# The program's beginning of a two-layer decoder: c spread into PSUM, six modulation rows on TensorE

## The chip, the cores and the metric

One core of one Trainium2 chip runs the whole program, as one launch. The time is device microseconds (us), the median of several executions.

## The reference, cut to what matters

Two layers (HGRN2, then forgetting attention), each followed by a squared-ReLU MLP, over 512 tokens of width 1024 in float32. Every sub-layer begins with an RMSNorm whose result is scaled and shifted by values that come from one conditioning vector c:

```python
c_act = jax.nn.silu(c)
for i in range(DEPTH):
    mod = c_act @ w_mod[i] + b_mod[i]          # (1, 6 * 1024)
    sh1, sc1, g1, sh2, sc2, g2 = jnp.split(mod, N_MOD, axis=-1)
    h = rmsnorm(x, norm1_w[i]) * (1 + sc1[:, None, :]) + sh1[:, None, :]
    ...
    proj = h @ w_in                            # hgrn2: q, fz, i, g
```

For the first projection the program thus needs the norm of x, and of `mod` the 1024 shifts sh1 and the 1024 scales sc1.

## The kernel before, in words

Activations lie transposed: tile `x` has 128 partitions by 8 feature blocks (k = 0 to 7) by 512 tokens. A weight comes as blocks of 128x1024 (512 KB). Products are made to near float32 accuracy out of a high and a low part: a matmul of `whi` with `h0hi`, of `whi` with `h0lo` and of `wlo` with `h0hi` (lines 704 to 706, 128x512 each), so that every block and every k costs three matmuls. ScalarE makes the high part of a weight block (`whi`), VectorE or GpSimd the low part (`wlo`).

Each engine has its order written out by hand, and semaphores join them. The DMA queue of SyncE loads in program order: c spread over all partitions (`cb`), the parameters (`par`), x, then the rows of w_mod in `modf` (first_rows(k) loads rows k and 8 + k), among them the first four weight blocks.

The beginning, up to the first projection's four blocks (`together`), works in these steps:

- The norm. ScalarE squares the eight blocks of x (L377), VectorE adds seven of them into `acc` (L1278), TensorE sums over partitions with matmuls of one column (`norm_0`, L732 and L736), VectorE adds epsilon (L1171), GpSimd takes the root (`root`, L648), TensorE spreads it over the partitions into a PSUM bank (L741).
- The modulation. Row m of `modf` holds, in partition p, the 1024 weights of output 128 m + p, so an output is a dot product along the free dimension with the silu of c in `cb`. VectorE takes the 8 shifts and the first 3 scales (L1262, `first_dots`), the other 5 scales are a product on GpSimd (L656) and a sum on ScalarE (L388). VectorE then adds the bias (L1268) and makes the gain (L1270).
- h0 itself, block by block of k: `t_of_0` (L1176, x times gain times root, the root read from PSUM) into one of two `scr` buffers; ScalarE adds the shift and rounds (L383, `h0hi`); `lower_0` (L1181) is the low part.
- TensorE waits for `h_lo` of k and runs 12 matmuls (four blocks by three).

GpSimd has in its queue, in this order: eight constants, seven masks (built in `scr[1]`, L626 to L636), the root, the low parts of the first four weight blocks (`lo`, L644), the five products of scales. VectorE waits for `masked` before `t_of_0(0)`.

After the four blocks come the value blocks of the next quad (L795 to L797), then the HGRN2 levels (`hg_core`), which other code orders. SyncE's queue goes on with a wait on `w_lo` before each reload of a weight buffer.

Of the kernel before, what the change touches and what calls it, by code (L numbers as in the profile page):

```python
# [13 lines left out]
P = 128  # L14
T = 512
# [23 lines left out]
C_ALL = C_BMOD + 96  # L39
# [3 lines left out]
SPLITS = 10  # L43


def build(nc, x_t, c_row, stream, mod_rows, w_forget, params, out_t):
    keep = ExitStack()
    with keep:
# [15 lines left out]
        dots = sb("dots", [P, 4], F32)  # L64
        qkw = sb("qkw", [P, 1], F32)
# [16 lines left out]
        lbc = sb("lbc", [P, 6 * KT], F32, layer0)  # L82

# [3 lines left out]
        modf = sb("modf", [P, 2 * KT, D], F32, head0)  # L87
        head0.close()
# [39 lines left out]
        x_in = [sem(f"x_in{i}") for i in range(2)]  # L128
        par_in, wf_in, c_in = (sem(n) for n in ("par_in", "wf_in", "c_in"))
        modf_in = [sem(f"modf_in{i}") for i in range(KT)]  # L130
# [5 lines left out]
        cact = sem("cact")  # L136
# [8 lines left out]
        n_sum, n_var, n_rst, n_bc = (sem(n) for n in ("n_sum", "n_var", "n_rst", "n_bc"))  # L145
        h_t, h_hi, h_lo = (sem(n) for n in ("h_t", "h_hi", "h_lo"))
# [21 lines left out]
        SHARED = 3  # L168

# [6 lines left out]
        SQ_AT = {1: 8, 2: 20, 3: 30, 4: 42}  # L176
        ADD_AT = {1: 7, 2: 16, 3: 23, 4: 32}
# [101 lines left out]
        def _(sp):  # L279
            sp.dma_start(cb[:, :], c_row.partition_broadcast(P)).then_inc(c_in, 16)  # L280
            sp.dma_start(par[:, :], params).then_inc(par_in, 16)
            for i in range(2):
                sp.dma_start(x[:, 4 * i:4 * i + 4, :], x_t[:, 4 * i:4 * i + 4, :]).then_inc(x_in[i], 16)
            def first_rows(k):

                rows = mod_rows[0:2 * KT].rearrange("(h m) p k -> p h m k", h=2)
                sp.dma_start(modf[:, :, :].rearrange("p (h m) k -> p h m k", h=2)[:, :, k, :],
                             rows[:, :, k, :]).then_inc(modf_in[k], 16)
# [52 lines left out]
        def _(act):  # L341
# [259 lines left out]
        def _(pool):  # L601
# [17 lines left out]
            n = 6  # L619
            for lv in range(MASKED):  # L620
                pool.wait_ge(gp, n)
                if lv:
                    m = 1 << (lv - 1)
                    nb = P // (2 * m)
                    v = scr[1][:, 0:P].rearrange("p (b h m) -> p b h m", h=2, m=m)
                    G.memset(v[:, :, 0, :], 0.0)  # L626
                    G.memset(v[:, :, 1, :], 1.0).then_inc(gp, 1)

                    pool.wait_ge(gp, n + 1)
                    G.affine_select(out=v[:, :, 1, :], in_=v[:, :, 1, :], compare_op=ALU.is_ge, fill=0.0,  # L630
                                    base=0, pattern=[[-2 * m, nb], [0, m]], channel_multiplier=1).then_inc(gp, 1)
                    pool.wait_ge(gp, n + 2)
                    G.affine_select(out=v[:, :, 1, :], in_=v[:, :, 1, :], compare_op=ALU.is_gt, fill=0.0,
                                    base=m, pattern=[[2 * m, nb], [0, m]], channel_multiplier=-1).then_inc(gp, 1)
                    pool.wait_ge(gp, n + 3)
                    G.tensor_copy(masks[:, lv, :], scr[1][:, 0:P]).then_inc(gp, 1)  # L636
                    n += 4
            pool.wait_ge(gp, n)
            G.memset(scr[1][:, 0:1], 0.0).then_inc(masked, 1)
# [11 lines left out]
            for j in range(4):  # L651
                lo(0, j)
            pool.wait_ge(cact, 1)
            for k in range(SHARED, KT):
                pool.wait_ge(modf_in[k], 16)
# [40 lines left out]
        def _(pe):  # L696
# [29 lines left out]

            def norm_0():
# [94 lines left out]
            def together(jobs, h, ready):  # L822

                for k in range(KT):
                    pe.wait_ge(h_lo, ready + k + 1)
                    for quad, j, bank in jobs:
                        if k == 0:
                            split(quad, j)
# [877 lines left out]
```

## Time and profile before

| | us |
|---|---|
| median of 3 runs (lowest 1471.47, highest 1475.01) | 1474.58 |
| the profiled execution | 1476.3 |
| its span, first to last instruction | 1474.5 |
| TensorE matmul busy in the span | 1399.3 (95%) |
| VectorE busy | 774.9 (53%) |
| ScalarE busy | 501.6 (34%) |
| GpSimd busy | 162.5 (11%) |
| mean granted TensorE clock | 0.979 |

The page of the profile gives the busy time of each engine over the whole span and then in 40 slices of 37 us. Of the first slice PE is busy two tenths, VectorE seven, GpSimd eight, and the DMA engines nine; of every later slice PE is busy eight tenths or more, and the last has seven. Times of the trace run from the span's start. The page calls TensorE PE, VectorE DVE, ScalarE ACT, GpSimd POOL and SyncE SP. A matmul of 4-byte operands that are not fp32r (the sums, the spreads, the dots) is listed as two instructions, each with its own load of the stationary operand, so that x8 stands for four of them in the code.

### The profile page before, as it was taken

How to read it: one execution, taken by the hardware profiler on the slowest of the kernel's cores; microseconds unless marked ns; L12 is line 12 of the kernel's file. 1: busy time of each engine (PE TensorE's matmuls, PEld its weight loads, DVE VectorE, ACT ScalarE, POOL GpSimd, SP SyncE). 2: the span in 40 equal slices, each digit the busy share in tenths (PEclk: the TensorE clock that was granted, in tenths of full speed). 3: DMA queues.
4: the chain of work that ended last, by engine and by line, in shares of the span. 5: the costliest groups of instructions: out<-in, count | busy, mean ns of one | idle time of the engine just before them, and what ended most of it. 6: DMA issues, size and time to landing. Idle time of an engine off the chain costs nothing.

```text
span 1474.5 us, 21837 instructions
## 1 busy us (share of the span) xinstructions
PE 1399.3 (95%) x8152; PEld 1217.8 (83%) x8152; DVE 774.9 (53%) x1348; ACT 501.6 (34%) x771; POOL 162.5 (11%) x199
## 2 busy tenths in 40 slices
PE   2899999999999999999998898998999999999997
PEld 2688988989988888888997797987899888888887
DVE  7865757565775556653464454454466433244323
ACT  3423232413443223332253444444344322133220
POOL 8242415050000000000020101010000000000000
PEclk9899999999999999999999999999999999999999
DMA  9243334322365446542232121211023322323221
GB/s 374 100 167 130 116 115 140 119 72 58 106 243 179 171 180 230 189 170 85 73 105 97 57 87 58 86 51 51 29 86 101 100 86 85 108 92 99 88 69 58
DMA packets 47224, 169.95 MB, mean 115 GB/s; under 512 B 5025, under 2 KB 7201, under 8 KB 46385
## 3 DMA queue, kind: packets, MB, share of 16 engines
q1 hardware_dynamic: 46544, 164.73, 32.7%
q10 hardware_dynamic: 608, 4.23, 0.7%
q8 instruction: 50, 0.82, 0.2%
q14 instruction: 22, 0.17, 0.0%
HBM read 166.81 MB, written 2.13 MB: 115 GB/s over the span
## 4 chain that ended last, share of the span: by engine, by line
PE 87%; DVE 6%; ACT 4%; issue 2%; DMA 1%; POOL 0%; POOLq 0%; DVEq 0%; ACTq 0%; SPq 0%
PE bank L704 21%; PE bank L705 21%; PE bank L706 21%; PE bank L795 3%; PE bank L797 3%; PE bank L796 3%; PE bank L870 3%; PE bank L1066 2%; PE bank L1052 1%; PE bank L889 1%; PE bank L1034 1%; DVE modf L1262 1%; ACT whi L346 1%; ACT L587 1%; ACT L526 1%
## 5 line engine op out<-in xcount | busy, mean ns | idle before, releaser
L346 ACT ACTIVATE whi<-raw 128x1024 fp32r<-128x1024 f32 x204 | 215.2, 1055 | 267.7 <-PE bank L706 252.2
L1223 DVE TENSOR_TENSOR wlo<-raw,whi 128x1024 fp32r<-128x1024 f32 x204 | 251.4, 1246 | 17.1 <-ACT whi L346 17.1
L648 POOL TENSOR_TENSOR rst<-ssq,mhalf 128x2 f32<-128x2 f32 (+3 forms) x21 | 39.8, 1893 | 1166.7 <-DVE ssq L1171 954.2
L1471 DVE TENSOR_TENSOR scr<-scr 128x512 f32<-128x512 f32 x64 | 44.3, 692 | 124.9 <-ACT scr L494 124.9
L704 PE MATMUL bank<-h1hi,whi 128*128 128x512 f32 (+1 forms) x288 | 107.4, 373 | 0.8 <-DVE h1lo L1203 0.7
L704 PE MATMUL bank<-h3hi,whi 128*128 128x512 f32 (+1 forms) x288 | 107.5, 373 | 0.7 <-DVE h3lo L1203 0.6
L705 PE MATMUL bank<-h1lo,whi 128*128 128x512 f32 (+1 forms) x288 | 107.4, 373 | 0.0
L705 PE MATMUL bank<-h3lo,whi 128*128 128x512 f32 (+1 forms) x288 | 107.1, 372 | 0.0
L706 PE MATMUL bank<-h3hi,wlo 128*128 128x512 f32 (+1 forms) x288 | 107.1, 372 | 0.0
L704 PE MATMUL bank<-a1hi,whi 128*128 128x512 f32 (+1 forms) x288 | 106.6, 370 | 0.0
L705 PE MATMUL bank<-a1lo,whi 128*128 128x512 f32 (+1 forms) x288 | 106.5, 370 | 0.0
L706 PE MATMUL bank<-a1hi,wlo 128*128 128x512 f32 (+1 forms) x288 | 106.5, 370 | 0.0
L705 PE MATMUL bank<-a0lo,whi 128*128 128x512 f32 (+1 forms) x288 | 106.1, 369 | 0.0
L706 PE MATMUL bank<-h1hi,wlo 128*128 128x512 f32 (+1 forms) x288 | 106.0, 368 | 0.0
L704 PE MATMUL bank<-a0hi,whi 128*128 128x512 f32 (+1 forms) x288 | 105.8, 368 | 0.0
L706 PE MATMUL bank<-a0hi,wlo 128*128 128x512 f32 (+1 forms) x288 | 104.8, 364 | 0.0
L494 ACT ACTIVATE scr<-bank 128x512 f32<-128x512 f32 x64 | 38.2, 597 | 189.8 <-PE bank L706 189.7
L1214 DVE CUSTOM_DVE_ANT_0 mring<-mring,cb 128x1024 f32<-128x1024 f32 x80 | 98.6, 1240 | 1.5 <-DMA mring<-mod_rows 1.5
L704 PE MATMUL bank<-h0hi,whi 128*128 128x512 f32 x192 | 82.4, 429 | 14.4 <-DVE h0lo L1181 14.1
L795 PE MATMUL bank<-whi,h2hi 128*128 128x256 f32 x320 | 95.6, 299 | 0.0
L797 PE MATMUL bank<-wlo,h2hi 128*128 128x256 f32 x320 | 91.6, 286 | 0.0
L796 PE MATMUL bank<-whi,h2lo 128*128 128x256 f32 x320 | 91.4, 286 | 0.0
(249 smaller groups left out, 3161.0 us busy)
## 6 DMA issues: line engine op xcount, KB each, us to landing
raw<-stream SPq DMA_DIRECT2D x208, 512.0 KB, 4.1
mring<-mod_rows SPq DMA_DIRECT2D x80, 512.0 KB, 3.5
modf<-mod_rows SPq DMA_DIRECT2D x8, 1024.0 KB, 18.0
fb<-negf ACTq DMA_DIRECT2D x4, 1024.0 KB, 5.7
x<-x_t SPq DMA_DIRECT2D x2, 1024.0 KB, 7.9
out_t<-x SPq DMA_DIRECT2D x8, 256.0 KB, 2.2
cb<-c_row SPq DMA_DIRECT2D x1, 512.0 KB, 4.5
wf<-w_forget SPq DMA_DIRECT2D x1, 512.0 KB, 5.7
```

Of the source, the lines that this page charges most:

```text
L346: S.activation(whi[:, j, :], raw[:, j, :], ACT.Copy).then_inc(w_hi, 1)
L648: G.tensor_tensor(rst[:, at:at + n], ssq[:, at:at + n], mhalf[:, 0:n], ALU.pow).then_inc(done, 1)
L704: PE.matmul(out, wh, hh[0], start=first, stop=False)
L705: PE.matmul(out, wh, hh[1], start=False, stop=False)
L706: return PE.matmul(out, wl, hh[0], start=False, stop=last)
L795: PE.matmul(o, hh, whi[:, j, w0], start=k == 0 and t % 2 == 0, stop=False, skip_group_check=True)
L796: PE.matmul(o, hl, whi[:, j, w0], start=False, stop=False, skip_group_check=True)
L797: mm = PE.matmul(o, hh, wlo[:, j, w0], start=False, stop=k == KT - 1, skip_group_check=True)
L870: mm = PE.matmul(second_halves(cols(ps[j], t), m), cols(kk, t), second_halves(cols(qq, t), m), start=True, stop=True)
L1214: V.tensor_tensor_reduce(out=mring[:, s, :], in0=mring[:, s, :], in1=cb[:, :], scale=1.0, scalar=0.0, op0=ALU.mult, op1=ALU.add, accum_out ...
L1223: V.tensor_tensor(wlo[:, j, :], raw[:, j, :], whi[:, j, :].bitcast(F32), ALU.subtract).then_inc(w_lo, 1)
L1471: V.tensor_tensor(scr[j % 2][:, :], scr[j % 2][:, :], scr[j % 2][:, :], ALU.mult).then_inc(ff_sq, 1)
```

## The change

- `cb` is no longer loaded. c comes as 8 columns of `par`; ScalarE takes their silu (`csil`), TensorE spreads it into the banks 0 and 1 (`spread_c`), where VectorE's dots read it; ScalarE copies it to `cb` for GpSimd's products and for everything later.
- The norm's squares are shared: ScalarE the even blocks, VectorE the odd ones, added in pairs; TensorE sums each pair apart (20 matmuls of one column where there were 8).
- Six rows (scales 0 to 3, shifts 0 and 1) are laid out on the host as weight blocks, and TensorE takes their dots: `row_dot`, 8 matmuls of one column each. Three stand before the first product, three between the first blocks.
- VectorE keeps x times the root in `xn`. ScalarE makes the modulated value with scale and bias (one more pass) and then its high part; VectorE's low part is a plain difference of two SBUF tiles.
- Shifts 2 to 7 are dots of VectorE in halves against PSUM, with the bias as their start value; scales 4 to 7 stay with GpSimd and ScalarE.
- GpSimd builds masks in a tile of its own, three before the root and four between the low parts and the scales; VectorE makes the low part of block 0.
- Each row of w_mod and each quarter of x is loaded by itself, scale row before shift row, the weight blocks between them.

PE from its first instruction, before (a bank name leaves out its number; `acc` and `scr` are sums of squares, `rst` is the root):

```order
L732 MATMUL bank<-meand,acc 128x1 [waits x_acc,consts]
L732 MATMUL bank<-meand,acc 128x1 x3
L736 MATMUL bank<-meand,scr 128x1 [waits x_sq]
L736 MATMUL bank<-meand,scr 128x1 x3
L741 MATMUL bank<-ident,rst 128x128 [waits n_rst]
L741 MATMUL bank<-ident,rst 128x128 x3
L704 MATMUL bank<-h0hi,whi 128x512 [waits w_lo,w_hi,h_lo]
```

and now, from the sum of the last pair on:

```order
L778 MATMUL bank<-meand,acc 128x1 [waits sq0,add0]
L778 MATMUL bank<-meand,acc 128x1 x3
L778 MATMUL bank<-meand,scr 128x1 x4
L796 MATMUL bank<-csil,modf 128x1 [waits n_var,modf_in8]
L796 MATMUL bank<-csil,modf 128x1 x7
L785 MATMUL bank<-ident,rst 128x128 [waits n_rst]
L785 MATMUL bank<-ident,rst 128x128 x3
L796 MATMUL bank<-csil,modf 128x1 [waits mv_used,n_var,modf_in0]
L796 MATMUL bank<-csil,modf 128x1 x7
L796 MATMUL bank<-csil,modf 128x1 [waits h_t,n_var,modf_in9]
L796 MATMUL bank<-csil,modf 128x1 x7
L738 MATMUL bank<-h0hi,whi 128x512 [waits w_lo,w_hi,h_lo]
```

Three dots stand between the sums and the first product; ahead of these rows are 8 matmuls of the spread of c and 12 of sums.

DVE where the third block of h0 is made (k = 2), before:

```order
L1262 ISA modf,mod<-modf,cb 128x1024 [waits modf_in2]
L1262 ISA mod 128x1
L1262 ISA modf,mod<-modf,cb 128x1024
L1262 ISA mod 128x1
L1268 TENSOR_TENSOR mod<-mod,par 128x1 [waits dv]
L1268 TENSOR_TENSOR mod<-mod,par 128x1
L1270 SCALAR_TENSOR_TENSOR gain<-mod,par 128x1 [waits dv]
L1176 SCALAR_TENSOR_TENSOR scr<-x,gain,bank 128x512 [waits h_lo,dv]
L1181 SCALAR_TENSOR_TENSOR h0lo<-scr,mod,h0hi 128x512 [waits h_hi]
```

and now, from the gain of k = 2 to the low part of the same k:

```order
L1327 TENSOR_SCALAR gain<-bank,small,par 128x1 [waits mv]
L1347 ISA modf,part_dot<-modf,bank,par 128x512 [waits modf_in2,c_bc]
L1347 ISA part_dot 128x1
L1347 ISA modf,mod<-modf,bank,part_dot 128x512 [waits dv]
L1347 ISA mod 128x1
L1233 TENSOR_TENSOR xn<-x,bank 128x512
L1327 TENSOR_SCALAR gain<-bank,small,par 128x1 [waits mv]
L1347 ISA modf,part_dot<-modf,bank,par 128x512 [waits modf_in3]
L1347 ISA part_dot 128x1
L1347 ISA modf,mod<-modf,bank,part_dot 128x512 [waits dv]
L1347 ISA mod 128x1
L1237 TENSOR_TENSOR h0lo<-scr,h0hi 128x512 [waits h_hi]
```

The low part of k = 2 stands behind the wait for `mv` of the sixth dot and behind the shift dot of k = 3.

The diff, cut to its core:

```diff
 @block.sync
...
-    sp.dma_start(cb[:, :], c_row.partition_broadcast(P)).then_inc(c_in, 16)
...
+    for i in range(4):
+        sp.dma_start(x[:, 2 * i:2 * i + 2, :], x_t[:, 2 * i:2 * i + 2, :]).then_inc(x_in[i], 16)
+    def first_rows(m):
+        sp.dma_start(modf[:, m, :], mod_rows[m]).then_inc(modf_in[m], 16)
...
+    for k in range(KT):
+        first_rows(KT + k)
+        if k < 2:
+            weight(0, 2 * k)
         first_rows(k)
+        if k < 2:
+            weight(0, 2 * k + 1)
...
+    S.activation(csil[:, :], par[:, C_C:C_C + KT], ACT.Silu).then_inc(cact, 1)
     act.wait_ge(lb_mx, 1)
...
+    for i in range(4):
+        act.wait_ge(x_in[i], 16)
+        if i >= 2:
+            act.wait_ge(add0, i - 1)
+        S.activation(scr[i % 2][:, :], x[:, 2 * i, :], ACT.Square).then_inc(sq0, 1)
+    act.wait_ge(c_bc, 1)
+    for i in range(2):
+        S.activation(cb[:, T * i:T * i + T], ps[i][:, :], ACT.Copy).then_inc(cb_in, 1)
+    def first_hi(j):
+        act.wait_ge(raw_in[j], 16)
+        S.activation(whi[:, j, :], raw[:, j, :], ACT.Copy).then_inc(w_hi, 1)
+    def upper_0(k):
         act.wait_ge(h_t, k + 1)
+        if k >= 2:
+            act.wait_ge(h_lo, k - 1)
+        else:
+            act.wait_ge(n_sum, 1)
+        S.activation(scr[k % 2][:, :], xn[:, k, :], ACT.Identity, scale=gain[:, k:k + 1],
+                     bias=mod[:, SH1 + k:SH1 + k + 1]).then_inc(h_32, 1)
+        act.wait_ge(h_32, k + 1)
+        S.activation(h0[0][:, k, :], scr[k % 2][:, :], ACT.Copy).then_inc(h_hi, 1)
+    first_hi(0)
+    first_hi(1)
+    upper_0(0)
+    first_hi(2)
+    first_hi(3)
+    for k in range(1, KT):
+        if k >= SCALES:
+            m = KT + k
+            act.wait_ge(scale_mul, k - SCALES + 1)
             S.activation(modf[:, m, :], modf[:, m, :], ACT.Copy,
                          accum_out=mod[:, m:m + 1]).then_inc(scale_sum, 1)
+        upper_0(k)
...
     root(n_var, 1, TT, n_rst)
+    pool.wait_ge(w_lo, 1)
+    for j in range(1, 4):
         lo(0, j)
+    for lv in range(4, MASKED):
+        mask(lv)
+    pool.wait_ge(gp, at_gp[0])
+    G.memset(mtmp[:, 0:1], 0.0).then_inc(masked, 1)
+    pool.wait_ge(cb_in, 2)
+    for k in range(SCALES, KT):
+        pool.wait_ge(modf_in[KT + k], 16)
         G.tensor_tensor(modf[:, KT + k, :], modf[:, KT + k, :], cb[:, :], ALU.mult).then_inc(scale_mul, 1)
...
+    def spread_c():
+        pe.wait_ge(cact, 1)
+        for k in range(KT):
+            mm = PE.matmul(cols(ps[k // 4], k % 4), csil[:, k:k + 1].broadcast_to([P, P]), ident[:, :],
+                           start=True, stop=True)
+        mm.then_inc(c_bc, 1)
     def norm_0():
+        sums = NORM0_BANKS[0]
+        for i in range(4):
+            pe.wait_ge(add0, i + 1)
+            if i == 3:
+                pe.wait_ge(sq0, 4)
+            for a in ((sqb, acc)[i % 2], scr[1])[:2 if i == 3 else 1]:
+                for t in range(TT):
+                    mm = PE.matmul(sums[:, t:t + 1], cols(a, t), meand[:, 0:1], start=i == 0 and t == 0,
+                                   stop=i == 3, skip_group_check=True)
+            mm.then_inc(sq0_used if i < 3 else n_sum, 1)
+    def spread_0():
         pe.wait_ge(n_rst, 1)
         for t in range(TT):
...
         mm.then_inc(n_bc, 1)
+    def row_dot(n, m):
+        pe.wait_ge(modf_in[m], 16)
+        pe.wait_ge(n_var, 1)
+        if n:
+            pe.wait_ge((h_t, mv_used)[n % 2], (n + 1) // 2)
+        for k in range(KT):
+            mm = PE.matmul(NORM0_BANKS[0][:, 16 + m:17 + m], cols(modf[:, m, :], k), csil[:, k:k + 1],
+                           start=k == 0, stop=k == KT - 1, skip_group_check=True)
+        mm.then_inc(mv, 1)
...
+    spread_c()
     norm_0()
+    row_dot(0, SC1)
+    spread_0()
+    row_dot(1, SH1)
+    row_dot(2, SC1 + 1)
...
-    together([(0, j, 4 + j) for j in range(4)], h0, 0)
+    later_dots = {(0, 1): (3, SH1 + 1), (0, 2): (4, SC1 + 2), (1, 1): (5, SC1 + 3)}
+    for k in range(KT):
+        pe.wait_ge(h_lo, k + 1)
+        for j in range(4):
+            if k == 0:
+                split(0, j)
+            mm = product(ps[4 + j][:, :], j, k, [h0[0][:, k, :], h0[1][:, k, :]], k == 0, k == KT - 1)
+            if k == KT - 1:
+                mm.then_inc(pe_blk, 1)
+            if (k, j) in later_dots:
+                row_dot(*later_dots[k, j])
...
+    def normed_0(k):
+        V.tensor_tensor(xn[:, k, :], x[:, k, :], NORM0_BANKS[1][:, :], ALU.mult)
...
     def lower_0(k):
         dve.wait_ge(h_hi, k + 1)
+        V.tensor_tensor(h0[1][:, k, :], scr[k % 2][:, :], h0[0][:, k, :].bitcast(F32),
+                        ALU.subtract).then_inc(h_lo, 1)
...
+    for i in range(4):
+        dve.wait_ge(x_in[i], 16)
+        if i >= 2:
+            dve.wait_ge(sq0_used, i - 1)
+        b = (sqb, acc)[i % 2][:, :]
+        ins = V.tensor_tensor(b, x[:, 2 * i + 1, :], x[:, 2 * i + 1, :], ALU.mult)
+        if i < 3:
+            link(ins)
+            dve.wait_ge(sq0, i + 1)
+            ins = V.tensor_tensor(b, b, scr[i % 2][:, :], ALU.add)
+        ins.then_inc(add0, 1)
...
+    def first_gain(k, total):
+        return V.tensor_scalar(gain[:, k:k + 1], total, small[:, 24 + k:25 + k], par[:, C_N1 + k:C_N1 + k + 1],
+                               ALU.add, ALU.mult)
+    def gain_of_row(n, k):
+        dve.wait_ge(mv, n + 1)
+        return first_gain(k, NORM0_BANKS[0][:, 16 + SC1 + k:17 + SC1 + k]).then_inc(mv_used, 1)
+    def shift_of_row(n, k):
+        dve.wait_ge(mv, n + 1)
+        at = C_BMOD + SH1 + k
+        V.tensor_scalar(mod[:, SH1 + k:SH1 + k + 1], NORM0_BANKS[0][:, 16 + SH1 + k:17 + SH1 + k],
+                        par[:, at:at + 1], None, ALU.add).then_inc(h_t, 1)
+    def shift_dot(k):
+        dve.wait_ge(modf_in[SH1 + k], 16)
+        to = (part_dot[:, k:k + 1], mod[:, SH1 + k:SH1 + k + 1])
+        at = C_BMOD + SH1 + k
+        for i in range(2):
+            half = modf[:, SH1 + k, T * i:T * i + T]
+            ins = V.tensor_tensor_reduce(out=half, in0=half, in1=ps[i][:, :], scale=1.0,
+                                         scalar=(par[:, at:at + 1], to[0])[i], op0=ALU.mult, op1=ALU.add,
+                                         accum_out=to[i])
+            if i == 0:
+                link(ins)
+        return ins
     dve.wait_ge(n_sum, 1)
     eps_var(NORM0_BANKS[0][:, 0:TT], TT).then_inc(n_var, 1)
-    first_dots(1)
+    lower(0, 0)
+    gain_of_row(0, 0)
     dve.wait_ge(n_bc, 1)
+    normed_0(0)
+    shift_of_row(1, 0)
+    normed_0(1)
+    lower_0(0)
+    gain_of_row(2, 1)
+    shift_of_row(3, 1)
+    normed_0(2)
+    lower_0(1)
+    gain_of_row(4, 2)
+    dve.wait_ge(c_bc, 1)
+    shift_dot(2).then_inc(h_t, 1)
+    normed_0(3)
+    gain_of_row(5, 3)
+    shift_dot(3).then_inc(h_t, 1)
+    lower_0(2)
+    for k in range(4, KT):
+        normed_0(k)
+        shift_dot(k)
+        lower_0(k - 1)
+        dve.wait_ge(scale_sum, k - SCALES + 1)
+        first_gain(k, mod[:, SC1 + k:SC1 + k + 1]).then_inc(h_t, 1)
+    lower_0(KT - 1)
     dve.wait_ge(masked, 1)
+    dve.wait_ge(cb_in, 2)
...
+for m in list(range(SHIFTS)) + [KT + k for k in range(SCALES)]:
+    mod_rows[m] = feature_block(i["w_mod"][0], m)
```

SHIFTS is 2 and SCALES is 4. The lines that the diff takes out are in the listing of the kernel before, by the numbers named above.

## Rows read from the trace of the kernel before

**Rows 1.** The chain of waits, 0 to 110 us: start us, us, what
```profile
28.80 3.31 DVE modf L1262
...
35.47 2.25 DVE mod L1268 x2
```

**Rows 2.** The timeline of PE: start us, us, engine, line, operation
```profile
15.33 1.84 PE L732 MATMUL bank<-meand,acc 128*128 128x1 f32 x8 [15.33 <-DVE acc L1278]
17.03 1.85 PE L736 MATMUL bank<-meand,scr 128*128 128x1 f32 x8
21.22 2.07 PE L741 MATMUL bank<-ident,rst 128*128 128x128 f32 x8 [2.35 <-POOL rst L648]
28.85 0.79 PE L704 MATMUL bank<-h0hi,whi 128*128 128x512 f32 x1 [5.55 <-DVE h0lo L1181]
29.44 0.63 PE L705 MATMUL bank<-h0lo,whi 128*128 128x512 f32 x1
...
42.83 0.80 PE L704 MATMUL bank<-h0hi,whi 128*128 128x512 f32 x1 [8.58 <-DVE h0lo L1181]
...
60.50 0.51 PE L704 MATMUL bank<-h0hi,whi 128*128 128x512 f32 x1
...
65.89 0.40 PE L706 MATMUL bank<-h0hi,wlo 128*128 128x512 f32 x1
```

**Rows 3.** The timeline of DVE
```profile
5.58 0.25 DVE L1244 TENSOR_TENSOR small<-par 128x8 f32<-128x8 f32 x1 [5.58 <-DMA par<-params]
...
9.64 0.76 DVE L1278 TENSOR_TENSOR acc<-acc,sqb 128x512 f32<-128x512 f32 x1
...
39.97 0.75 DVE L1176 SCALAR_TENSOR_TENSOR scr<-x,gain,bank 128x512 f32<-128x512 f32 x1
40.64 2.14 DVE L1181 SCALAR_TENSOR_TENSOR h0lo<-scr,mod,h0hi 128x512 fp32r<-128x512 f32 x1
...
46.13 0.23 DVE L1268 TENSOR_TENSOR mod<-mod,par 128x1 f32<-128x1 f32 x2
...
47.25 0.74 DVE L1181 SCALAR_TENSOR_TENSOR h0lo<-scr,mod,h0hi 128x512 fp32r<-128x512 f32 x1
47.91 1.22 DVE L1262 CUSTOM_DVE_ANT_0 modf<-modf,cb 128x1024 f32<-128x1024 f32 x1
```

**Rows 4.** The timeline of POOL
```profile
2.62 0.15 POOL L626 MEMSET scr<- 128x64 f32 x1
...
16.57 0.10 POOL L639 MEMSET scr<- 128x1 f32 x1
...
21.15 9.88 POOL L644 TENSOR_TENSOR wlo<-raw,whi 128x1024 fp32r<-128x1024 f32 x4
30.99 14.02 POOL L656 TENSOR_TENSOR modf<-modf,cb 128x1024 f32<-128x1024 f32 x5
```

**Rows 5.** The timeline of ACT
```profile
17.54 1.06 ACT L380 ACTIVATE whi<-raw 128x1024 fp32r<-128x1024 f32 x1 [2.49 <-DMA raw<-stream]
18.82 1.06 ACT L380 ACTIVATE whi<-raw 128x1024 fp32r<-128x1024 f32 x1 [0.22 <-DMA raw<-stream]
...
47.37 0.72 ACT L383 ACTIVATE h0hi<-scr,mod 128x512 fp32r<-128x512 f32 x1 [4.85 <-DVE scr L1176]
```

**Rows 6.** Windows of PE: stretch, us, busy (instructions), granted clock, DMA share, GB/s
```profile
46.00:48.00 2.00, 2.00 (x6) 0.58 0.00 0
...
90.00:92.00 2.00, 2.00 (x7) 0.50 0.00 0
92.00:94.00 2.00, 2.00 (x14) 0.99 0.00 0
```

**Rows 7.** The timeline of PE, 80 to 94 us
```profile
85.42 3.65 PE L870 MATMUL bank<-hq,hk 128*128 128x64 f32 x16 [2.55 <-DVE adiag L1323]
88.82 0.77 PE L704 MATMUL bank<-h0hi,whi 128*128 128x512 f32 x1
```

**Rows 8.** Groups of DVE by form: count, busy us, mean ns
```profile
L1525 DVE CUSTOM_DVE_ANT_0 scr<-bank,fb 128x512 f32<-128x512 f32 x16 | 11.0, 686 | 17.9 <-issue 17.9
```

More of the change, by code:

```diff
@@ L127, in build @@
         pe_blk = sem("pe_blk")
-        x_in = [sem(f"x_in{i}") for i in range(2)]
-        par_in, wf_in, c_in = (sem(n) for n in ("par_in", "wf_in", "c_in"))
-        modf_in = [sem(f"modf_in{i}") for i in range(KT)]
+        x_in = [sem(f"x_in{i}") for i in range(4)]
+        par_in, wf_in = sem("par_in"), sem("wf_in")
+        modf_in = [sem(f"modf_in{i}") for i in range(2 * KT)]
         mod_in = [sem(f"mod_in{i}") for i in range(2)]
@@ L166, in build @@
         out_t_ready, out_done = sem("out_t_ready"), sem("out_done")
-        SHARED = 3
         TH = T // 2
@@ L725, in half_block @@
                 return mm
-            def norm_0():
-                sums, spread = NORM0_BANKS
-                pe.wait_ge(x_acc, KT - 1)
-                for t in range(TT):
-                    PE.matmul(sums[:, t:t + 1], cols(acc, t), meand[:, 0:1], start=t == 0, stop=False,
-                              skip_group_check=True)
-                pe.wait_ge(x_sq, KT)
-                for t in range(TT):
-                    mm = PE.matmul(sums[:, t:t + 1], cols(scr[0], t), meand[:, 0:1], start=False, stop=True,
-                                   skip_group_check=True)
-                mm.then_inc(n_sum, 1)
+            def spread_c():
[4 more added lines that the diff above has]
+                mm.then_inc(c_bc, 1)
@@ L820, in hg_half @@
                     quarter_token(n, i - 12, 4 if g else 2, h0)
[L822 to L828, printed above, removed]
-                        mm = product(ps[bank][:, :], j, k, [h[0][:, k, :], h[1][:, k, :]], k == 0, k == KT - 1)
-                        if k == KT - 1:
-                            mm.then_inc(pe_blk, 1)
-            together([(0, j, 4 + j) for j in range(4)], h0, 0)
+            later_dots = {(0, 1): (3, SH1 + 1), (0, 2): (4, SC1 + 2), (1, 1): (5, SC1 + 3)}
[9 more added lines that the diff above has]
+                        row_dot(*later_dots[k, j])
             for i in range(12, 16):
@@ L1273, in _ @@
-            link(V.memset(acc[:, :], 0.0))
-            for k in range(KT - 1):
-                dve.wait_ge(x_sq, k + 1)
-                if k:
-                    dve.wait_ge(x_acc, k)
-                V.tensor_tensor(acc[:, :], acc[:, :], (sqb, scr[0])[k % 2][:, :], ALU.add).then_inc(x_acc, 1)
-            dve.wait_ge(cact, 1)
-            first_dots(0)
+            V.tensor_scalar(small[:, 24:32], par[:, C_BMOD + SC1:C_BMOD + SC1 + KT], 1.0, None, ALU.add)
+            for i in range(4):
[9 more added lines that the diff above has]
+                ins.then_inc(add0, 1)
```

125 lines of the change are left out of this document (38 added, 87 removed).

## The prediction, made before the changed kernel ran

> **What bounds the kernel now.** Read the 40 slices first: PE is busy in every slice but the first. A change to the beginning can therefore only move the moment from which PE is never long without work.
>
> The chain of waits says what holds that moment back: up to 60 us it hardly runs over PE, but over VectorE's dots, its tiny additions and the low parts [rows 1]. As the mark I take the end of the four blocks, whose last matmul starts at 65.89 and ends at 66.3 [rows 2]; what follows is unchanged and moves with it. In PE's timeline the groups of 12 matmuls begin at 28.85 (k = 0), 42.83 (k = 1) and 60.50 (k = 6), and k = 6 and 7 run back to back, 2.8 us each [rows 2]. So the last wait that counts is that for k = 6.
>
> The timeline of DVE shows why k = 1 is so late. An addition of one element takes 0.23/2 us at 46.13, but a pair took 2.25 at 35.47 [rows 1, 3]. A dot takes 1.14 to 1.22 alone and 3.31 in the chain at 28.80; the low part 0.74 alone and 2.14 at 40.64. The slow ones all read two SBUF tiles and fall into the 24 us in which POOL multiplies tiles of 1024 (21.15 to 45.0) [rows 4]. The operation at 39.97, whose second tile is in PSUM, takes its 0.75 in the middle of that. This stall, about 14 us between 28.8 and 42.8, is what the change goes for. Behind 46 the pace is 3.1 us for each k, without stall.
>
> **The price list on PE.** A matmul of one column with a 4-byte stationary tile is two instructions; eight instructions take 1.70 from start to start (15.33 to 17.03) [rows 2]. So a sum over a pair (4 matmuls) costs 1.70, a row's dot (8 matmuls) 3.41, the spread of the root 1.8, the spread of c 3.6. That price belongs to the low clock. The trace shows it in the wide matmuls that come next: 0.59 and then 0.43 us from start to start for 512 columns: 28.85 to 29.44, and twelve in the 5.4 us up to the next wait. From 60.50 to 65.89 the same 24 matmuls stand 0.23 apart [rows 2]. 512 columns in 0.43 us is the 1.2 GHz level, 0.23 nearly the 2.4 GHz level. When does the clock rise? The granted clock went up at 47.7, after 4.9 us of nothing but wide matmuls from 42.83 on, and at about 92.0, after 3.2 us of them from 88.82 on [rows 2, 6, 7]. Before the latter PE had run 16 instructions of 64 columns without a gap for 3.65 us, at the low price, and the clock had stayed at 0.50 [rows 6, 7]. So I expect the clock at its low level as long as dots and sums stand between the wide matmuls: the dots of rows run at 1.2 GHz.
>
> **The change, step by step**, in us of the trace.
>
> - *Loads.* `par` landed at 5.58, queued behind the 512 KB of `cb` [rows 3]. Blocks of 512 KB land 1.28 apart (17.54, 18.82) [rows 5]. Less that, and less 0.45 for an issue earlier, gives 3.9 (bounds 3.1 and 5.1). Then every 512 KB 1.28: scale row 0 at 10.3, the last row of all at 34.6. Each is used later than this below: the loads cost nothing, and removing `cb` brings only the earlier start.
> - *Norm.* Before, the first addition of squares came 4.06 behind `par` (5.58 to 9.64) [rows 3]. Now a square of VectorE comes first, but the table load of ScalarE is no longer behind `cb`; I take 4.3, so PE's first sum at 8.2. The spread of c (3.9 + 0.3 + 3.6 = 7.8) is just done. Five sums of 1.70 back to back: 16.7. VectorE's squares and additions (0.7 each) keep ahead of them. Before, the sums ended at 18.9 (17.03 + 1.85): 2.2 earlier, although 20 matmuls replace 8.
> - *Up to the first product.* Epsilon 0.2, dot of scale 0 3.4: 20.3. Spread of the root 1.8 (the root itself lies beside the dot): 22.1. Dot of shift 0: 25.5. VectorE's addition 0.2, dot of scale 1: 29.1. The h0 of k = 0 is ready at 25.7 + 1.4 (two passes of ScalarE of 0.72 and less [rows 5]) + 0.7 = 27.8 and waits. First product at 29.1, before 28.85: what the norm won, the dots have spent.
> - *The blocks of k = 0 and 1.* A block costs 3 x 0.43 = 1.3 and 0.15 more behind a dot (0.59 instead of 0.43). So 30.5; dot 34.0; block 35.4; dot 38.8; the four blocks up to 44.1 (k = 1 begins in their middle, at 41.5, before at 42.83); dot of scale 3 47.5; two blocks 50.2. The h0 of k = 1 follows the fourth dot by 0.2 + 1.4 + 0.7, so it is there at 36.3.
> - *VectorE behind that.* Its queue holds the gain of k = 3 (waits for the sixth dot, 47.5), then the shift dot of k = 3, then the low part of k = 2. A half dot with PSUM is 0.69 plus its read; a form like it is in [rows 8]. Started one behind the other, two come to 1.5. So shift 3 at 49.2, low part of k = 2 at 49.9 (PE is free at 50.2), low part of k = 3 at 49.9 + 0.7 + 1.5 + 0.7 = 52.8.
> - *k = 4 to 7.* For each, 0.7 (`xn`) + 1.5 + 0.7 + 0.2 (gain) = 3.15 with its waits; before it was 3.1. The low part of k = 6 is at 52.8 + 3 x 3.15 = 62.2. That of k = 7 takes gain, 1.4 of ScalarE and 0.7: 64.5.
> - *PE.* Wide matmuls only from 47.5 on, so by those two cases the clock rises between 50.7 and 52.4. k = 2 ends near 53.8, k = 3 to 5 at 62.1, k = 6 starts at 62.2 instead of 60.50.
> - *What hides.* POOL: the low parts of blocks 2 and 3 need ScalarE at 28.2 and 29.3 and take 2.5 each [rows 4]: 33.1, against 38.8 needed. Four masks are 4/7 of 14.0: 41.1; four scale products of at most 2.8: 52.3, and their last sum on ScalarE at 53.5, against 62. If that cover of 9 us went (see the first rival), POOL would set the pace. The last weight reload and SyncE's wait for `mod_used` stay in their order. `cb` is complete by 12.
>
> **Sum.** Measured at the start of each group: k = 0 0.3 later, k = 1 1.3 earlier, k = 6 1.7 later, and k = 6 and 7 take 5.5 as before, so +1.7 at the mark. The 14 us of stall at the port are gone, and in their place stand five dots of 3.4 that only PE's queue delays (two before the first product, besides the one that covers the root, and three behind it). Against the profiled 1476.3 that is 1478.0. This execution lay 1.7 above the median of the runs shown, so the median after should be **1476.3**. Unknown costs: landing of `par` -0.8 to +1.2; the pace of k = 4 to 7 -0.5 to +0.5; the clock may already rise within the four blocks from 38.9 to 44.1 (5.1 us of wide matmuls, against 3.2 to 4.9 seen), the sixth dot is then 1.7 and all later is 1.7 earlier. Own range 1473.5 to 1479. A measurement of this kernel can tell about 0.3% (4.4 us) from no change.
>
> **The rivals.**
>
> *The narrow matmuls raise the clock.* PE has work almost without pause from 4.2 us on. At 2.4 GHz from the third sum on, sums cost 0.85, dots 1.7: sums end at 14.2, first product at 21.5, sixth dot at 31.0. VectorE would be ready with scale 4 at 36.5, but POOL (masks until 35, a product each 3.2 with VectorE's low parts in between) has the last one at 47.8. End of k = 7 about 54, 12 before the old one: 1462.5. The Trainium skill, in "TensorE: Matmul & The Clock Gate", Part 1, speaks for it: "the default state is throttled, and activity releases the throttle", whatever the number of matmuls. By that rule the time would be the one just given. Against it stands the 0.50 of the stretch at 90, behind 3.65 us of narrow ones [rows 6, 7]. Chance 0.20.
>
> *A lucky clock.* The rise within the four blocks (-1.7), and in addition no fall of the clock around 85, where PE waits 2.55 us and then runs 6.7 us at the low level [rows 7]; half of that, 3.4, can go if all is shifted: 1474.6 + 1.7 - 1.7 - 3.4 = 1471.2. Chance 0.15.
>
> *Slower: dots dilute the wide matmuls.* Place: k = 2 and 3. If the clock rises in the four blocks and falls again over the sixth dot and the wait behind it, or never rises before 60, then both groups cost 5.1 instead of 2.8 or less: 50.2 + 10.3 = 60.5, four more of 2.8 end at 71.6, 5.3 behind the old 66.3: 1474.6 + 5.3 = 1479.9. It decides from the point where the low clock lasts beyond 57. For it: in the stretch at 85 the clock stayed low behind narrow matmuls, and here they stand between the wide ones. Against: two rises within 4.9 us. Chance 0.13.
>
> *The change doesn't relieve VectorE* (its PSUM operands wait for POOL all the same): the 0.75 at 39.97 excludes it almost wholly, and it would only add to the rival before.
>
> **How the numbers follow.** Forecast 0.52, rivals 0.20, 0.15 and 0.13. Faster by over 0.3% needs less than 1470.2: the first rival and a quarter of the second, 0.24. Slower, above 1479.0: most of the third and the edge of the forecast, 0.14. Within: 0.62. The range goes from 1464 to 1480.5: it holds the forecast, the second and third cases and the slower edge of the first, of which some 0.15 stays out, too far off to take in.
>
> **What would show it.** In PE's timeline after: sums 1.70 apart and dots of 3.4 (first rival: 0.85 and 1.7); the first product near 29, the group of k = 6 near 62; the small additions of VectorE at 0.2 throughout; the granted clock at low level until 50 to 52. Wrong I am if the first product stands before 26, if a dot takes under 3, or if the order of waits on VectorE puts the low part of k = 2 anywhere but behind the sixth dot.

## The result: slower by 0.65%, and not where the change is

| | before | changed |
|---|---|---|
| median of 5 runs, us | 1474.58 | 1483.98 (1481.62 to 1486.01) |
| ratio, 95% interval | 1 | 1.0065 (1.0046 to 1.0084) |
| profiled execution, us | 1476.3 | 1481.68 |

The forecast was no change, 1476.3, with a range of 1464 to 1480.5; the kernel became 9.4 us slower. The profiled execution of the changed kernel is the second fastest of its five and that of the kernel before the slowest, so the traces differ by only 5.4 us of span. A ratio here and below comes from all the runs together and can differ a little from the quotient of two medians.

The timeline of PE of the changed kernel, in its beginning (start us, us, engine, line, operation), answers to [rows 2]:

```profile
7.10 1.16 PE L778 MATMUL bank<-meand,sqb 128*128 128x1 f32 x8 [0.21 <-DVE sqb L1322]
...
14.73 3.55 PE L796 MATMUL bank<-csil,modf 128*128 128x1 f32 x16 [0.35 <-DVE ssq L1230]
...
27.20 0.77 PE L738 MATMUL bank<-h0hi,whi 128*128 128x512 f32 x1
...
39.30 0.63 PE L738 MATMUL bank<-h0hi,whi 128*128 128x512 f32 x1
...
41.70 1.84 PE L796 MATMUL bank<-csil,modf 128*128 128x1 f32 x16
...
46.44 0.50 PE L738 MATMUL bank<-h0hi,whi 128*128 128x512 f32 x1 [1.39 <-DVE h0lo L1237]
...
63.17 0.40 PE L740 MATMUL bank<-h0hi,wlo 128*128 128x512 f32 x1
```

The last matmul of the four blocks (the prediction's mark) starts at 63.17; before it was 65.89. So in this execution the beginning, all that the change is about, is 2.7 us **faster**. The first product stands at 27.20 (28.85 before), k = 1 at 39.30 (42.83), and behind the 1.39 us wait at 46.44, where k = 2 starts, PE never waits again until the mark. The slow operations of VectorE are gone but for one low part. Its timeline:

```profile
45.23 1.16 DVE L1237 TENSOR_TENSOR h0lo<-scr,h0hi 128x512 fp32r<-128x512 f32 x1
...
54.06 0.69 DVE L1237 TENSOR_TENSOR h0lo<-scr,h0hi 128x512 fp32r<-128x512 f32 x1
...
56.92 0.69 DVE L1237 TENSOR_TENSOR h0lo<-scr,h0hi 128x512 fp32r<-128x512 f32 x1
```

The low part at 45.23 took 1.16 while GpSimd was still multiplying (until 45.84), where before one took 2.14 and a dot 3.31 [rows 1, 3]; the later ones (54.06, 56.92) take 0.69 and come 2.86 apart. In two further profiles of this beginning (a_128 and a_pad160, below) the same low part took 2.33 and 2.66, so this remnant of the stall is not always as small as here.

**Where the time is lost** is seen if the same instruction is looked up in both traces. Before, in the timeline of ACT (same columns):

```profile
64.31 1.06 ACT L346 ACTIVATE whi<-raw 128x1024 fp32r<-128x1024 f32 x1 [3.77 <-PE bank L706]
...
284.53 0.63 ACT L432 ACTIVATE y0hi<-scr 128x512 fp32r<-128x512 f32 x1 [6.89 <-DVE scr L1349]
...
430.66 0.60 ACT L494 ACTIVATE scr<-bank 128x512 f32<-128x512 f32 x1 [3.41 <-PE bank L706]
...
600.96 0.60 ACT L494 ACTIVATE scr<-bank 128x512 f32<-128x512 f32 x1 [3.41 <-PE bank L706]
...
644.90 0.60 ACT L494 ACTIVATE scr<-bank 128x512 f32<-128x512 f32 x1 [3.40 <-PE bank L706]
...
710.82 1.06 ACT L346 ACTIVATE whi<-raw 128x1024 fp32r<-128x1024 f32 x1 [4.43 <-PE bank L706]
```

and changed, the same instructions in the same order (601.0 and 644.9 before, eight blocks apart, answer to two rows that are nine blocks apart here):

```profile
61.55 1.06 ACT L352 ACTIVATE whi<-raw 128x1024 fp32r<-128x1024 f32 x1 [2.21 <-PE bank L740]
...
283.97 0.63 ACT L458 ACTIVATE y0hi<-scr 128x512 fp32r<-128x512 f32 x1 [7.18 <-DVE scr L1439]
...
430.56 0.60 ACT L520 ACTIVATE scr<-bank 128x512 f32<-128x512 f32 x1 [3.54 <-PE bank L740]
...
599.25 0.60 ACT L520 ACTIVATE scr<-bank 128x512 f32<-128x512 f32 x1 [3.54 <-PE bank L740]
...
649.85 0.60 ACT L520 ACTIVATE scr<-bank 128x512 f32<-128x512 f32 x1 [3.53 <-PE bank L740]
...
717.33 1.06 ACT L352 ACTIVATE whi<-raw 128x1024 fp32r<-128x1024 f32 x1 [4.57 <-PE bank L740]
```

The lead of 2.76 us at 64 us is 0.56 at 284 and 0.10 at 431; at 711 it is a lag of 6.51. It doesn't go in a wait: from 431 us on it goes evenly. Each row of line 494 before (520 now) empties a finished block of 24 products of 512 columns. Before, eight blocks take 43.94 us, **5.49** each; now nine take 50.60, **5.62** each. 51 blocks between 431 and 711 at 0.13 are the 6.6 us. PE has no idle time there and no low clock; the windows of PE for 400 to 700 us (stretch, its length, busy time and matmuls, granted clock, DMA share, GB/s), first of the kernel before, then of the changed one:

```profile
400.00:700.00 300.00, 300.00 (x1325) 1.00 0.52 182
```
```profile
400.00:700.00 300.00, 300.00 (x1292) 1.00 0.52 181
```

The same granted clock of 1.00 (the 2.4 GHz level), the same DMA share, and each matmul takes 5.4 ns longer from start to start (5.62 and 5.49 us over 24). These instructions are the same in both programs. Such a thing had no place in my forecast. Behind 711 us the difference wanders (it is 5.4 at the end); that part is not explained, and one profile of each kernel cannot carry it.

### The profile page after: what moved, and what is told of

It is laid out like the page before. It is cut to its first block, busy times and chain, and to the rows that moved or that the text cites. A ratio compares the mean times of both kernels' runs of the same rounds, so it can differ in the third digit from the quotient of the medians.

```text
span 1479.9 us, 22111 instructions
## 1 busy us (share of the span) xinstructions
PE 1430.7 (97%) x8288; PEld 1239.9 (84%) x8288; DVE 752.5 (51%) x1337; ACT 504.4 (34%) x775; POOL 152.4 (10%) x197
## 4 chain that ended last, share of the span: by engine, by line
PE 90%; DVE 4%; ACT 4%; issue 2%; DMA 0%; POOL 0%; POOLq 0%; SPq 0%; DVEq 0%; ACTq 0%
PE bank L738 21%; PE bank L739 21%; PE bank L740 21%; PE bank L855 3%; PE bank L857 3%; PE bank L856 3%; PE bank L929 3%; PE bank L1125 2%; PE bank L1111 1%; PE bank L796 1%; PE bank L948 1%; ACT whi L352 1%; PE bank L1093 1%; DVE wlo L1277 1%; ACT L613 1%
## 5 line engine op out<-in xcount | busy, mean ns | idle before, releaser
L1454 DVE SCALAR_TENSOR_TENSOR x<-bank,mod,x 128x256 f32<-128x256 f32 (+1 forms) x44 | 26.5, 603 | 121.1 <-PE bank L740 120.8
```

## The experiments

**What could stretch an unchanged matmul?** The diff adds `csil` and `part_dot` (32 bytes a partition each) ahead of the large tiles and makes `par` 32 bytes wider. Tiles are allocated one behind the other, so everything from `mring` on moves up by 96 bytes, in the first layer by 608 with `mtmp`. `x`, `raw`, `whi` and `wlo` stand ahead and stay. In every product of these stages a slice of h or a is the weight tile (stationary) and a row of `whi` or `wlo` is moved past it. The weight tiles lay on a multiple of 64 bytes before and lie 32 past one now. All experiments but the last two change only that.

### The kernel before with the changed kernel's addresses

```diff
         acc = sb("acc", [P, T], F32)
+        pad = sb("pad", [P, 24], F32)
```

> The kernel before, with one tile of 96 bytes a partition (24 f32 columns, never used) allocated behind acc. Nothing else differs: every tile from mring on lies 96 bytes higher, so that the tiles that serve as weights (h0 to h3, a0, a1) start at 32 past a multiple of 64 bytes, as they do in the changed kernel, and not at a multiple of 64. Theory A (addresses): the 512-column products of the first layer's feed-forward stage step at 0.2343 us each in place of 0.2288, the last ones of the second layer at 0.2333 in place of 0.2325, and the whole becomes 8 to 12 us slower, 1483 to 1487 us. Rival B (the time is lost by the new instructions of the beginning, their place in TensorE's program or the order of the loads): 1474.6 us and steps of 0.2288. Rival C (chance of the chip or its clock): steps differ from run to run for the same kernel.

Measured: 1484.52 us against 1474.05, ratio 1.0073 (1.0050 to 1.0097): the whole loss of the change, from one tile that nobody uses. Its ACT timeline has the blocks of the changed kernel:

```profile
596.08 0.60 ACT L495 ACTIVATE scr<-bank 128x512 f32<-128x512 f32 x1 [3.43 <-PE bank L707]
...
652.31 0.60 ACT L495 ACTIVATE scr<-bank 128x512 f32<-128x512 f32 x1 [3.53 <-PE bank L707]
```

Ten blocks in 56.23 us, 5.62 each. Theory A holds, and B, new instructions, isn't needed: there are none here. C, chance, falls: the six runs lie between 1480.40 and 1485.55, all above the slowest of the 23 of the kernel before (1477.63). A triple of products (`h1hi` with `whi`, `h1lo` with `whi`, `h1hi` with `wlo`) takes 0.703 us from start to start, 0.687 before.

### The changed kernel, back on multiples of 64

The same line with `[P, 8]` in the changed kernel.

> The changed kernel with one unused tile of 32 bytes a partition behind acc, which puts the weight tiles of both layers back on multiples of 64 bytes (first layer 640 bytes above the kernel before, second layer 128). Theory A: the steps fall to 0.2288 us in the first layer's feed-forward stage, the beginning keeps the 2.7 us that it gained at the last product of the four blocks, and the whole is 1471 to 1473 us. Rival B: 1484 us and steps of 0.2343, as in the changed kernel. Rival C: either, and not the same from run to run.

Measured: 1473.87 us, ratio 1.0012 (0.9994 to 1.0029). The loss is gone, but not for the reason given: the first layer's blocks are still slow, and the second layer's have become faster than they ever were.

```profile
599.28 0.60 ACT L521 ACTIVATE scr<-bank 128x512 f32<-128x512 f32 x1 [3.51 <-PE bank L741]
...
649.68 0.60 ACT L521 ACTIVATE scr<-bank 128x512 f32<-128x512 f32 x1 [3.51 <-PE bank L741]
...
1205.75 1.06 ACT L353 ACTIVATE whi<-raw 128x1024 fp32r<-128x1024 f32 x1 [4.29 <-PE bank L741]
...
1271.03 1.06 ACT L353 ACTIVATE whi<-raw 128x1024 fp32r<-128x1024 f32 x1 [4.30 <-PE bank L741]
```

5.60 each for nine blocks in the first layer (5.49 expected), and 65.28 us for twelve, **5.44** each, in the second (5.58 before). So the rest modulo 64 is not the rule.

### Multiples of 64, but the other ones

`[P, 16]` in the kernel before.

> The kernel before with 64 unused bytes behind acc: weight tiles stay on multiples of 64, but those of the first layer go from 64 past a multiple of 128 to a multiple of 128, and those of the second layer the other way. Theory A1 (only the rest modulo 64 counts): no change, 1474.6 us, steps of 0.2288 and 0.2325. Theory A2 (the rest modulo 128 counts, which would explain why the second layer steps at 0.2325 and the first at 0.2288 in the kernel before): the first layer goes to 0.2325, the second to 0.2288, and the whole is some 2 to 6 us slower. Rivals B and C: no change of the steps.

Measured: 1478.48 us, ratio 1.0034 (1.0020 to 1.0047); blocks of 5.58 in the first layer and 5.60 in the second. A1 falls. A2 is right for the first layer and wrong for the second, which it had at 5.49. Modulo 256 instead of 128 all eight values so far fit: the first layer of this kernel and the second of the kernel before both lie at rest 0 and both have 5.58; the first of a_pad32 and the second of this one both lie at 64 and have 5.60.

### Same addresses, both programs

Now both beginnings can be compared with the addresses equal: once with the rests modulo 256 that the kernel before has, twice with rest 128, at which `whi` and `wlo` lie. In the changed kernel the former takes `[P, 40]` behind `acc`. The latter is

```diff
 (kernel before)
         acc = sb("acc", [P, T], F32)
+        pad = sb("pad", [P, 32], F32)
...
         lbc = sb("lbc", [P, 6 * KT], F32, layer0)
+        pad0 = sb("pad0", [P, 16], F32, layer0)
```

and in the changed kernel `[P, 8]` behind `acc` and `[P, 16]` behind `mtmp`.

> The changed kernel with 160 unused bytes a partition behind acc: the weight tiles of the first layer start at 192 past a multiple of 256 bytes and those of the second at a multiple of 256, which is where they start in the kernel before. Theory A (the weight tile's rest modulo 256 sets the step; 0.2289, 0.2323, 0.2343 and 0.2333 us at 192, 0, 32 and 96): steps of 0.2289 in the first layer and 0.2323 in the second, as before, and the whole is what the kernel before takes less the 2.7 us of the beginning, 1471 to 1472 us. Rival B (the new instructions cost time after the beginning): 1476 us or more, and a place after the four blocks where the lead of 2.7 us is lost.

> The kernel before with 128 unused bytes behind acc and 64 behind lbc: the weight tiles of both layers start at 128 past a multiple of 256, the rest at which whi and wlo lie and at which the second layer of a_pad32 stepped at 0.2267. Theory A with period 256: 0.2267 in both layers; some 830 triples of 512-column products in the first layer at 0.0067 us and 700 in the second at 0.017 us a triple less, 17 us, so 1457 us (1452 to 1462). Rival A2 (the period is longer than 256, or the layers differ for another reason): 0.2267 in the second layer only, 1462 us or more.

> The changed kernel with 32 unused bytes behind acc and 64 behind mtmp: the weight tiles of both layers at 128 past a multiple of 256, as in b_128. Theory A: steps of 0.2267 in both layers, and 2.7 us less than b_128: 1454 us (1449 to 1460). Rival B: not faster than b_128.

| addresses | kernel before | changed kernel |
|---|---|---|
| as before (192 and 0) | 1474.39 | 1475.57, ratio 1.0002 (0.9990 to 1.0015) |
| 128 and 128 | 1465.30, ratio 0.9934 (0.9917 to 0.9950) | 1464.25, ratio 0.9935 (0.9919 to 0.9950) |

All ratios are to the kernel before. The profile of b_128, both layers:

```profile
598.81 0.60 ACT L496 ACTIVATE scr<-bank 128x512 f32<-128x512 f32 x1 [3.35 <-PE bank L708]
...
642.33 0.60 ACT L496 ACTIVATE scr<-bank 128x512 f32<-128x512 f32 x1 [3.35 <-PE bank L708]
...
1202.29 1.06 ACT L348 ACTIVATE whi<-raw 128x1024 fp32r<-128x1024 f32 x1 [4.29 <-PE bank L708]
...
1267.57 1.06 ACT L348 ACTIVATE whi<-raw 128x1024 fp32r<-128x1024 f32 x1 [4.30 <-PE bank L708]
```

5.44 and 5.44. Two things follow. At equal addresses the changed beginning is worth **nothing that can be told from zero**, within 0.15% or 2.2 us, in place of the 2.7 us that both theories took from a single profile. And 0.65% lay in the addresses: a_128 and b_128 beat both kernels. I had expected 1457 and 1454. The first layer's blocks gained 0.05 as foreseen, but my 830 and 700 triples a layer counted those of the other stages at the full price, where going from 64 to 0 gains less (a triple of `h0` is 0.690 before and 0.687 here; in the changed kernel, at 160, it is 0.703, so those stages follow the distance too). With the 56 blocks of each layer's feed-forward stage alone (224 records of 512 columns in the group below, of the changed kernel, so 28 blocks of 8 for `a0`, and as many for `h1`), it is 56 x 0.053 + 56 x 0.137 = 10.6; measured 9.1.

```profile
L738 PE MATMUL bank<-a0hi,whi 128*128 128x512 f32 x224 | 88.8, 396 | 0.0
```

### The weight tile's own address, or its distance

```diff
         raw = sb("raw", [P, 4, D], F32)
+        padw = sb("padw", [P, 32], F32)
```

on top of a_128.

> As a_128, with 128 further unused bytes ahead of whi, so that whi, wlo and every tile behind them move up by 128 together: the distance between the weight tiles and the moved tiles is that of a_128, but each now starts at a multiple of 256. Theory R (the distance modulo 256 counts): steps of 0.2267 and the time of a_128. Theory S (the weight tile's own rest counts): steps of 0.2323 as at rest 0, some 20 to 30 us slower than a_128.

Measured: 1465.93 us (2 runs), ratio 0.9940 (0.9919 to 0.9961).

```profile
598.09 0.60 ACT L523 ACTIVATE scr<-bank 128x512 f32<-128x512 f32 x1 [3.35 <-PE bank L743]
...
641.61 0.60 ACT L523 ACTIVATE scr<-bank 128x512 f32<-128x512 f32 x1 [3.35 <-PE bank L743]
```

5.44: theory R. A weight tile on a multiple of 256 is fast beside a moved tile that also lies on one, and slow (5.58, in b_pad64 and in the second layer before) beside one at 128.

### The two distances still missing

`[P, 56]` behind `acc` in the kernel before.

> The kernel before with 224 unused bytes behind acc: the weight tiles of the first layer lie at 160 past a multiple of 256, those of the second at 224; against whi and wlo, which lie at 128, these are distances of 32 and 96, the two that no run has yet. Theory R (the distance from the moved tile to the weight tile, modulo 256, sets the step; measured so far for three products: 0.680 us at 0, 0.687 at 64, 0.697 at 128, 0.703 at 160, 0.700 at 192 and 224): between their neighbours if the step grows with the distance, 0.680 to 0.687 in the first layer and 0.687 to 0.697 in the second, so 1468 to 1475 us. Rival (what counts is only that both lie at the same rest modulo 64): about 0.700 in both, 1480 to 1484 us.

Measured: 1480.43 us, ratio 1.0051 (1.0030 to 1.0071), 5.60 in both layers. The rival is the nearer one: the step does not grow with the distance alone. All eight distances, as mean time of a block of 24 products (two rows of ACT's timeline 8 to 12 blocks apart, as above):

| weight tile less moved tile, bytes mod 256 | block, us | seen in |
|---|---|---|
| 0 | 5.44 | a_pad32 (2nd layer), b_128, a_128, a_128_all128 |
| 64 | 5.49 | before and a_pad160 (1st) |
| 128 | 5.58 | before and a_pad160 (2nd), b_pad64 (1st) |
| 192 | 5.60 | a_pad32 (1st), b_pad64 (2nd) |
| 32, 96, 224 | 5.60 | b_pad224 (1st, 2nd), changed and b_pad96 (2nd) |
| 160 | 5.62 | changed and b_pad96 (1st) |

A period longer than 256 doesn't fit: in b_128 the distance is 58112 bytes in the first layer and 44544 in the second, rests of 256 and 0 modulo 512, and both have 5.44.

### What the row dots cost

On top of a_128, in `row_dot`:

```diff
-                for k in range(KT):
+                for k in (0, KT - 1):
```

> As a_128, but each of the six row dots on TensorE issues 2 of its 8 accumulating groups (the other six eighths of each dot are left out, so six modulation values are partial sums). Measures what the dots cost in the beginning. Theory D (they hold the path at 1.2 GHz, 3.4 us each, and the one within the blocks keeps the clock low): first product 4 to 8 us earlier than a_128's 36.59 us, the last product of the four blocks at 58 to 61 us against 63.82, the whole 3 to 6 us less. Rival V (VectorE's period of 2.85 us from the fourth block step on sets the end of the blocks): at most 2 us less.

Measured: 1452.62 us (2 runs), 11.6 less than a_128. The timeline of PE:

```profile
16.47 0.98 PE L798 MATMUL bank<-csil,modf 128*128 128x1 f32 x4 [0.34 <-DVE ssq L1232]
...
20.27 0.85 PE L798 MATMUL bank<-csil,modf 128*128 128x1 f32 x4
21.52 0.98 PE L798 MATMUL bank<-csil,modf 128*128 128x1 f32 x4 [0.40 <-DVE mod L1339]
23.67 0.80 PE L740 MATMUL bank<-h0hi,whi 128*128 128x512 f32 x1 [1.16 <-DVE h0lo L1239]
...
26.39 0.85 PE L798 MATMUL bank<-csil,modf 128*128 128x1 f32 x4
...
28.53 0.85 PE L798 MATMUL bank<-csil,modf 128*128 128x1 f32 x4
...
33.10 0.50 PE L798 MATMUL bank<-csil,modf 128*128 128x1 f32 x4
...
53.93 0.39 PE L742 MATMUL bank<-h0hi,wlo 128*128 128x512 f32 x1
```

against a_128:

```profile
16.52 3.54 PE L798 MATMUL bank<-csil,modf 128*128 128x1 f32 x16 [0.34 <-DVE ssq L1232]
...
21.77 3.41 PE L798 MATMUL bank<-csil,modf 128*128 128x1 f32 x16
25.58 3.54 PE L798 MATMUL bank<-csil,modf 128*128 128x1 f32 x16 [0.40 <-DVE mod L1339]
28.99 0.77 PE L740 MATMUL bank<-h0hi,whi 128*128 128x512 f32 x1
...
31.69 2.29 PE L798 MATMUL bank<-csil,modf 128*128 128x1 f32 x16
...
34.62 2.12 PE L798 MATMUL bank<-csil,modf 128*128 128x1 f32 x16
...
40.07 1.84 PE L798 MATMUL bank<-csil,modf 128*128 128x1 f32 x16
...
63.82 0.39 PE L742 MATMUL bank<-h0hi,wlo 128*128 128x512 f32 x1
```

The six dots take 16.7 us there and 5.0 here, and of the 11.7 us between them 9.9 arrive at the last matmul of the mark (63.82 and 53.93). The first product comes 5.3 us earlier, 23.67 and 28.99; the 36.59 of my expectation is in truth the fourth block of k = 0. Theory D holds, and the price is higher than it said (58 to 61 for the last product, 3 to 6 us in all). How much of it is the dots' own length and how much the clock, which is fast earlier here, this run doesn't separate. V falls as a bound: it allowed 2 us. But with short dots its mechanism does appear. VectorE's low parts end at 42.80, 45.67 and 48.53, and k = 4, 5 and 6 start at 42.86, 45.72 and 48.59, so VectorE's pace of 2.87 us now sets that of PE; in a_128, whose k = 6 starts 1.3 us behind its low part, it doesn't.

The last dot alone, `(0, KT - 1) if n == 5 else range(KT)`:

> As a_128, but only the sixth row dot, the one between the products of the second 128 rows of the four blocks, is cut to 2 of its 8 groups (the rest of that one modulation value is left out). Theory D2 (this dot, narrow work among the first wide products, is what keeps the clock at 1.2 GHz until 52 to 55 us in some runs): the clock rises by 42 us and the last product starts by 63.0 us. Rival (the clock's phase is set by what came earlier and does not follow this dot): a last product anywhere from 63 to 67 us, as among the five profiles of the changed beginning so far.

Measured: 1463.01 us (2 runs), last product at 63.55, 0.3 earlier than in a_128. D2, which wanted 63.0 at the latest, missed: the granted clock was at 0.96 between 42 and 44 us, as it says, but 0.50 again between 46 and 48, and the last product stayed in the rival's span of 63 to 67. One profile doesn't prove the rival either.

## Why the prediction was wrong

**The step that failed is "what follows is unchanged and moves with it".** The instructions behind the mark are unchanged, their operands' addresses are not. The prediction gave the new tiles no term, that is nothing, without a reason; the runs show +10.5 us for their addresses alone (b_pad96, 1484.52 against 1474.05, ratio 1.0073), six times the +1.7 that its sum came to.

**For the beginning itself "no change that can be measured" was right, the steps to it less so.** Forecast +1.7 us at the mark and 1476.3; measured at equal addresses 1475.57, ratio 1.0002 (0.9990 to 1.0015, so -1.5 to +2.2 us). That +1.7 lies inside says little: nearly every step came earlier than forecast, by up to 4.4 us (k = 6 at 57.79 in the changed kernel against 62.2), and the mark 2.4 us earlier on the mean (65.2 against 67.6). Step by step:

- *Loads and norm.* Sums at 7.10 and ended at 14.4 (16.7 forecast): the first three took 1.05 to 1.16 in this execution, 1.84 to 1.87 in those of a_pad32 and a_128, where the sums ended at 15.9 and 16.2.
- *Row dots at 1.2 GHz, 3.4 us.* 3.41 in all those before the first product, as forecast. The stall of VectorE went, and these dots took its place: that was the heart of the forecast, and cutting them to a quarter gave back 9.9 us at the mark.
- *k = 1.* At 39.30, in a_pad160 at 37.73, forecast 41.5. *k = 2* at 46.44 and 48.10, forecast 50.2.
- *The last wait that counts.* I put it at k = 6, at 62.2, from a pace of VectorE of 3.15. It was 2.85, and PE waits last at k = 2. From there it runs at its own pace, so the mark hangs on the clock. That wait at k = 2 ends with a low part that the sum had at 0.7 and that took 1.16 to 2.66 beside GpSimd.
- *The clock.* I had it rise by 50.7 to 52.4. In the changed kernel the fifth and sixth blocks (k = 1) still stepped at 0.43, but the sixth dot (1.84 at 41.70) and the blocks behind it were fast: the rise came at about 41.5, within the four blocks, one of the unknown costs that the prediction names; in a_pad160 the step of 0.43 us lasts until 52.1. The last product of the mark started at 63.17, 66.68, 66.41, 63.82 and 65.81 in the five profiles of the full changed beginning, and within 65.42 to 65.89 in five of the old one: on the mean 0.5 earlier, with a spread of 3.5. A single profile of it can show 2.7 us of gain or a loss of 1. Some 0.4 us of that is the address again: the 60 products from k = 3 on step at 0.234 in the changed kernel and at 0.227 in a_128.

The windows of PE behind k = 2 show that spread, first a_pad160, then the changed kernel:

```profile
44.00:50.00 6.00, 4.37 (x11) 0.50 0.01 1
```
```profile
44.00:50.00 6.00, 4.61 (x20) 1.00 0.00 1
```

**The rivals.** That narrow matmuls raise the clock did not come true for the dots: PE was busy for 11.25 of the 12 us from 14 to 26 and the dots took 3.41 each. In the changed kernel the clock even went the other way: its first three sums took 1.05 to 1.16, the two behind them 1.85. The clock that sticks low into k = 2 and 3 happened in a_pad32 and a_pad160; with it the mark came 0.5 to 0.8 after the old one, not 5.3. Of the lucky clock the first half, a rise within the four blocks, happened in the changed kernel and in a_128; the second did not, since the clock was at 0.50 between 84 and 88 us in both. The change did relieve VectorE. None of the rivals had to do with what decided.

## What to carry to other kernels

A small tile that is added in front of large ones can be an edit to every matmul that reads them. When a kernel bound by TensorE changes its time evenly, with no new wait and the same clock, compare the step of one matmul in both traces, and the tile addresses, before looking at the edit. For products like these, a pad tile that makes weight tile and moved tile start at the same rest modulo 256 bytes a partition was worth 0.65%; and two versions are to be compared at equal rests.

## What the runs showed of the hardware

- A product of 512 columns of 4-byte data at the 2.4 GHz level stepped at 0.227 to 0.234 us depending on the distance of its two SBUF tiles, 3.4% from best to worst. The Trainium skill, "SBUF — State Buffer", section "Operand start alignment", lets a 4-byte operand start at any multiple of 4 and adds: "This is about legality, not speed". All tiles here obey it; the speed differs all the same. Why the distance counts the runs do not tell. That only the distance counts rests on one pair of kernels (a_128 and a_128_all128); only multiples of 32 were tried. The matmuls of 256 columns with the roles swapped were not measured well enough to say.
- The granted clock that the profile shows did not always tell the pace of TensorE in the first 31 us. Between 14 and 26 us a_pad160 (first) has 1.00 and the changed kernel 0.50:

```profile
14.00:26.00 12.00, 11.25 (x53) 1.00 1.03 410
```
```profile
14.00:26.00 12.00, 11.25 (x53) 0.50 1.03 410
```

Both have dots of 3.41 us in it, the price at the 1.2 GHz level. It isn't a matter of narrow matmuls: between 29 and 31 us a_pad160 runs products of 512 columns alone, 0.43 us apart, which is the 1.2 GHz level, and still shows 1.00:

```profile
29.00:31.00 2.00, 2.00 (x6) 1.00 0.99 395
```

So in such a stretch the step of a matmul is the measure. The Trainium skill, "TensorE: Matmul & The Clock Gate", Part 1, has the throttle released by activity; in these 12 us PE was busy for 11.25, and each dot still took 3.41.
- What is left open: why the first sums were fast in two of the five profiles and slow in three. It moves the first product (27.20 and 28.06 against 28.70 to 28.99) but doesn't order the marks: a_128 with slow sums has 63.82, a_128_all128, whose first two were fast, 65.81. No run tried it, and none tells what sets the moment at which the clock rises in the four blocks.
